# Sums and remainders at the entry of two feed-forward parts, moved from VectorE to GpSimd for three row pairs of four

## The reference

```python
# first block, after its mixer
x = x + jnp.einsum("bsc,cd->bsd", mix, w_out[l])
h = rms_norm(x, norm_ffn[l])
ff = jnp.square(jax.nn.relu(jnp.einsum("bsd,df->bsf", h, w_ff1[l])))
x = x + jnp.einsum("bsf,fd->bsd", ff, w_ff2[l])

# second block, after its mixer
mix = jnp.einsum('bsd,de->bse', merged, w_o)
x = layer_norm(ALPHA * x + mix, ln1_g, ln1_b)
hid = jax.nn.silu(jnp.einsum('bsd,df->bsf', x, w_gate)) * jnp.einsum('bsd,df->bsf', x, w_up)
ffn = jnp.einsum('bsf,fd->bsd', hid, w_down)
```

## Time and profile before

| | us |
|---|---|
| median of 3 runs | 2751.3 (2751.22 to 2753.59) |
| span of the profiled execution | 2749.3 |
| PE busy | 2639.2 (96%) |
| DVE busy | 1640.7 (60%) |
| ACT busy | 860.2 (31%) |
| POOL busy | 362.3 (13%) |

### The profile page before, as it was taken

One profiled execution on the slowest core, in us unless ns is written; L12 is line 12 of the kernel. 1 busy time (PEld: TensorE's weight loads), 2 busy tenths in 40 slices (PEclk: granted clock), 3 DMA queues, 4 the chain that ended last, 5 costly groups with the idle time before them and its releaser, 6 DMA issues. The chain is left out here.

```text
span 2749.3 us, 35644 instructions
## 1 busy us (share of the span) xinstructions
PE 2639.2 (96%) x14290; PEld 2108.7 (77%) x14290; DVE 1640.7 (60%) x2537; ACT 860.2 (31%) x1522; POOL 362.3 (13%) x191
## 2 busy tenths in 40 slices
PE   7999999999899999999999999999969999998998
PEld 5875558874488888888888888868967888887887
DVE  5894997771765655444783355323276666666446
ACT  4344444320444443111131222232143232323121
POOL 1212634420000000000011121144200000000000
PEclk9999999999899999999999999999989999999999
DMA  4011032230133337232121222262322222226131
GB/s 158 31 63 69 27 123 94 94 135 27 69 115 119 104 107 285 79 120 77 50 89 51 73 81 71 69 211 69 123 77 66 89 77 85 89 80 222 68 117 62
DMA packets 192627, 262.22 MB, mean 95 GB/s; under 512 B 15824, under 2 KB 121680, under 8 KB 192080
## 3 DMA queue, kind: packets, MB, share of 16 engines
q1 hardware_dynamic: 192464, 259.95, 28.0%
HBM read 196.80 MB, written 61.93 MB: 94 GB/s over the span
## 5 line engine op out<-in xcount | busy, mean ns | idle before, releaser
L1251 PE MATMUL ps<-gl_t,gl_slot 128*128 128x512 f32 x1056 | 243.0, 389 | 0.0
L1251 PEld LDWEIGHTS ps<-gl_t,gl_slot 128*128 128x128 f32 x1056 | 198.2, 188 | 41.2
L1251 PE MATMUL ps<-gl_b,gl_slot 128*128 128x512 f32 x768 | 182.7, 396 | 18.4 <-DVE gl_slot L3576 18.4
L1251 PE MATMUL ps<-w_hi,ff_hi 128*128 128x512 f32 x480 | 187.2, 390 | 0.0
L1251 PE MATMUL ps<-w_hi,ff_lo 128*128 128x512 f32 x480 | 186.8, 389 | 0.0
L1251 PE MATMUL ps<-w_lo,ff_hi 128*128 128x512 f32 x480 | 186.7, 389 | 0.0
L1251 PEld LDWEIGHTS ps<-gl_b,gl_slot 128*128 128x128 f32 x768 | 147.0, 192 | 50.1 <-issue 14.4
L1251 PE MATMUL ps<-ff_t,slot 128*128 128x512 f32 x768 | 179.3, 393 | 4.4 <-DVE ff_t L3017 4.4
L1251 PE MATMUL ps<-H_hi,tw_hi 128*128 128x512 f32 x448 | 175.6, 392 | 0.0
L1251 PE MATMUL ps<-H_rest,tw_hi 128*128 128x512 f32 x448 | 174.4, 389 | 0.0
L1251 PE MATMUL ps<-H_hi,tw_lo 128*128 128x512 f32 x448 | 174.3, 389 | 0.0
(11 more groups left out here) (420 smaller groups left out, 5678.2 us busy)
## 6 DMA issues: line engine op xcount, KB each, us to landing
wraw<-in_w_ff SPq DMA_DIRECT2D x32, 1024.0 KB, 5.9
ff_rows<-quad SPq DMA_DIRECT2D x64, 256.0 KB, 2.0
ff_raw<-ff_rows SPq DMA_DIRECT2D x7, 2048.0 KB, 7.9
traw<-in_w_in SPq DMA_DIRECT2D x28, 512.0 KB, 4.2
wq_raw<-in_w_in SPq DMA_DIRECT2D x6, 2048.0 KB, 8.6
wraw<-in_w_gate SPq DMA_DIRECT2D x22, 512.0 KB, 4.0
wraw<-in_w_up SPq DMA_DIRECT2D x22, 512.0 KB, 5.3
hid_rows<-gl_up SPq DMA_DIRECT2D x44, 256.0 KB, 2.0
```

The costliest lines, as they stand in the source:

```text
L1251: mm = nc.tensor.matmul(out_ap, stationary(a, k), moving(c, k), start=(k == 0 and n == 0), stop=(k == kts - 1 and n == 2))
```

## The change

For the row pairs 0, 1 and 2 of both entries, the two differences (t4 and t3 plain) and the four remainders leave DVE's queue and stand in POOL's, in the functions `pair_terms` and `gl_pair_terms`, with the same waits. For the last pair they stay on DVE (`last_terms`, `gl_last_terms`), right behind the lo of b22, as they stood. ACT's and PE's queues are as before, and so are the semaphores' counts.

```diff
+            def pair_terms(j):
+                hi_at = FEAT[0] + 7 * j + 2
+                cols, upper_cols = slice(P * j, P * j + P), slice(512 + P * j, 512 + P * j + P)
+                pool.wait_ge(sums_made, 3 * j + 1)
+                for h in (1, 0):
+                    G.tensor_tensor(half_plain[j][h], t2_plain, half_plain[j][h], ALU.subtract).then_inc(sums_made, 1)
+                pool.wait_ge(feat_hi, hi_at + 2)
+                G.tensor_tensor(ff_t1[:, 1, :, cols], t1_plain, ff_t1[:, 0, :, cols].bitcast(F32), ALU.subtract
+                                ).then_inc(terms_lo, 1)
+                pool.wait_ge(feat_hi, hi_at + 3)
+                pool.wait_ge(sums_made, 3 * j + 3)
+                G.tensor_tensor(ff_t4[:, 1, :, cols], half_plain[j][1], ff_t4[:, 0, :, cols].bitcast(F32), ALU.subtract
+                                ).then_inc(terms_lo, 1)
+                pool.wait_ge(feat_hi, hi_at + 4)
+                G.tensor_tensor(ff_t3[:, :, upper_cols], half_plain[j][0], ff_t3[:, :, cols].bitcast(F32), ALU.subtract
+                                ).then_inc(terms_lo, 1)
+                pool.wait_ge(feat_hi, hi_at + 5)
+                pool.wait_ge(terms_lo, 4 * j + 3)
+                G.tensor_tensor(ff_t2[:, j, 1], t2_plain, ff_t2[:, j, 0].bitcast(F32), ALU.subtract).then_inc(terms_lo, 1)
+            for j in range(3):
+                pair_terms(j)
...
                 elif q > 0:
                     term_sums(q // 2 - 1)
                     scale_row(q)
-                    rest_terms(q // 2 - 1)
...
             term_sums(3)
-            rest_terms(3)
+            last_terms(3)
...
                     gl_term_sums(t - 4)
-                    gl_rest_terms(t - 4)
+                    if t == NT - 1:
+                        gl_last_terms(t - 4)
```

More of the change, by code:

```diff
@@ L2558, in _, with gl_pair_terms @@
                 rest_wo(c)
+            def gl_pair_terms(j):
+                hi_at = FEAT[2] + 7 * j + 2
+                cols, upper_cols = slice(P * j, P * j + P), slice(512 + P * j, 512 + P * j + P)
+                pool.wait_ge(sums_made, GL_T_SUMS + 3 * j + 1)
+                for h in (1, 0):
+                    G.tensor_tensor(gl_half[j][h], gl_t2_plain, gl_half[j][h], ALU.subtract).then_inc(sums_made, 1)
+                pool.wait_ge(feat_hi, hi_at + 2)
+                G.tensor_tensor(gl_t1[:, 1, :, cols], gl_t1_plain, gl_t1[:, 0, :, cols].bitcast(F32), ALU.subtract
+                                ).then_inc(terms_lo, 1)
+                pool.wait_ge(feat_hi, hi_at + 3)
+                pool.wait_ge(sums_made, GL_T_SUMS + 3 * j + 3)
+                G.tensor_tensor(gl_t4[:, 1, :, cols], gl_half[j][1], gl_t4[:, 0, :, cols].bitcast(F32), ALU.subtract
+                                ).then_inc(terms_lo, 1)
+                pool.wait_ge(feat_hi, hi_at + 4)
+                G.tensor_tensor(gl_t3[:, :, upper_cols], gl_half[j][0], gl_t3[:, :, cols].bitcast(F32), ALU.subtract
+                                ).then_inc(terms_lo, 1)
+                pool.wait_ge(feat_hi, hi_at + 5)
+                pool.wait_ge(terms_lo, GL_TERMS + 4 * j + 3)
+                G.tensor_tensor(gl_t2[:, j, 1], gl_t2_plain, gl_t2[:, j, 0].bitcast(F32), ALU.subtract).then_inc(terms_lo, 1)
+            for j in range(3):
+                gl_pair_terms(j)
         @block.vector
@@ L2996, in term_sums, with last_terms @@
                                 ff_b22[:, :, P * j:P * j + P].bitcast(F32), ALU.subtract).then_inc(drained[b], 1)
+            def last_terms(j):
+                hi_at = FEAT[0] + 7 * j + 2
+                cols, upper_cols = slice(P * j, P * j + P), slice(512 + P * j, 512 + P * j + P)
                 dve.wait_ge(sums_made, 3 * j + 1)
@@ L2999, in term_sums @@
                 V.tensor_tensor(half_plain[j][0], t2_plain, half_plain[j][0], ALU.subtract).then_inc(sums_made, 1)
-            def rest_terms(j):
-                hi_at = FEAT[0] + 7 * j + 2
-                cols, upper_cols = slice(P * j, P * j + P), slice(512 + P * j, 512 + P * j + P)
                 dve.wait_ge(feat_hi, hi_at + 2)
@@ L3526, in gl_term_sums, with gl_last_terms @@
                                 gl_b22[:, :, P * j:P * j + P].bitcast(F32), sub).then_inc(drained[b], 1)
+            def gl_last_terms(j):
+                hi_at = FEAT[2] + 7 * j + 2
+                cols, upper_cols = slice(P * j, P * j + P), slice(512 + P * j, 512 + P * j + P)
                 dve.wait_ge(sums_made, GL_T_SUMS + 3 * j + 1)
@@ L3529, in gl_term_sums @@
                 V.tensor_tensor(gl_half[j][0], gl_t2_plain, gl_half[j][0], sub).then_inc(sums_made, 1)
-            def gl_rest_terms(j):
-                hi_at = FEAT[2] + 7 * j + 2
-                cols, upper_cols = slice(P * j, P * j + P), slice(512 + P * j, 512 + P * j + P)
                 dve.wait_ge(feat_hi, hi_at + 2)
```

## The result

The changed kernel takes 2756.75 us (median of 19 runs, 2754.32 to 2764.22) against 2751.55 us of the kernel before on the same chips (19 runs, 18 of them from 2749.05 to 2755.3, and one of 3008.72 that the median doesn't feel): ratio 1.002 with a 95% interval of 1.0014 to 1.0026. It is 5.2 us slower, just under the 0.2% that was set as the line, and so on the side that the prediction calls "same". The forecast was 2758.7, with 2752 to 2762 around it: the sign and the range held, the size was 7.4 instead of 5.2 us.

What follows compares the result with a forecast made beforehand. The loop over VectorE and ACT, not VectorE's busy time, was taken to bound the entries. First entry 2.8 plus second 4.6 gave 7.4 us: 2749.3 becomes 2756.7, the median 2.0 above it, 2758.7; range 2752 to 2762.

Steps and rivals of the forecast that it cites:

- What bounds: Both entries: PE waits for the loop over VectorE and ACT, 17.8 us per two tiles in the first, not VectorE's busy time.
- GpSimd's pace, 6.3 us from t2_plain to the cast: Each moved pair: five GpSimd instructions, 4 x 1.23 + 1.29 = 6.2 us, plus 0.1 hand-over, before ACT's cast of t2.
- Second entry, 1.9 + 2.7 = 4.6: Lo of the first weights 4.6 us later: 1.9 from late squares in pairs 0 and 1, 2.7 from pair 2's late cast.
- First entry, 2.8: First entry 2.8 us slower: 3 x 0.45 from late squares, plus one fall of the granted clock at 1.4.
- 0.45 late per pair: First entry: squares at 697.2 instead of 696.76, behind ACT's cast that waits for GpSimd, in each of three pairs.
- The price of the fall of the granted clock, 1.4: First entry: low clock after PE's new stall adds 1.4 us to the loop; possible in pairs 0 and 1, taken once.
- The collision itself: First entry: root and scaling instructions with two SBUF inputs wait for GpSimd's current instruction; small ones up to 1.2 us, scaling 2 or more.
- PE's new stall: First entry: PE waits some 2.5 us for the scaling before its turn, covered by losing the later 2.30 us stall.
- the first `ff_b` product 1.4 to 4.2 us later than 736.56: Sign for the changed profile: the first entry's first product comes 1.4 to 4.2 us later than 736.56.
- rival 1: VectorE and GpSimd don't meet in small instructions: first entry -3.0, second +4.6, together +1.6 us, 2752.9; chance 0.16.
- Rival 2: ACT isn't held, VectorE's freed time counts: 5.7 and 12.9 us gained, 2732.7, chance 0.05; in-between case 2747.1, chance 0.09.
- The chances: Whole kernel: slower by over about 0.2% (5.5 us) 0.55, same 0.40, faster 0.05.

Runs made afterwards that it cites:

- the kernel with pair 2 on VectorE: The move in the second entry only, pair 2 back on VectorE, GpSimd making pairs 0 and 1: 2753.5 us against 2750.7 of the kernel before.
- the kernel with t1 last: Both entries: differences on VectorE, GpSimd's t1 remainder after t4's and t3's; second entry: squares before t2's cast, pair 2 on VectorE. 2750.8 us against 2751.1 before.
- the kernel with t1 last in the second entry alone: Second entry only: differences on VectorE, t1's remainder after t4's and t3's, squares before t2's cast, pair 2 on VectorE. 2748.9 us against 2751.1 before.

## Why the prediction held, and where not

- **What bounds:** held. The loop over VectorE and ACT sets the entries, and of the 26 us of VectorE's time that was to be freed none came off.
- **GpSimd's pace, 6.3 us from t2_plain to the cast:** held, 2015.97 to 2022.38 is 6.4. The spacing of 1.23 in it was read from a multiplication (the eight rows of L2515), not, as the text says, from the same kind of subtraction; the subtractions then followed each other at 1.22 to 1.26.
- **Second entry, 1.9 + 2.7 = 4.6:** held. The length says 4.47, the kernel with pair 2 on VectorE 1.83 and so 0.92 for each of the others and 2.62 for pair 2.
- **First entry, 2.8:** this is the term that was mis-sized; it measured 0. Two steps of it failed. The squares "0.45 late per pair" were on time: I had let each small VectorE instruction hold GpSimd for 0.1, and the record shows GpSimd's first four instructions at 1.25 to 1.26, so the cast came at 696.2 in the time of before and not at 696.7. The price of the fall of the granted clock, 1.4, did not come: the stalls of 2.10 and 1.77 us left the turn at 1.09 and the next product at 7.03. The fall came behind the third stall, where it cost nothing. Both are seen in one execution of the changed kernel and in one of that with the first entry alone; that such a fall can cost the loop 1.7 us is shown by the kernel with t1 last.
- **The collision itself:** held, with its mechanism. Three small instructions at 0.66, 1.20 and 1.00 and the scaling at 2.25 were foretold ("up to 1.2", "2 us or more"), and they went when GpSimd was held back. What the scaling takes from GpSimd's remainder of t3, 1.0 us, reaches the cast and the squares. It eats what the earlier drain would have given, to within 0.03 us, and that the two are equal is luck: no row said so. The Trainium skill's page "SBUF — State Buffer", section "Who interferes with whom", which the prediction cites, also names VectorE's 2-port modes as meeting GpSimd, so the "only" in that sentence is too narrow; no run here shows such an instruction.
- **PE's new stall:** held, 2.10 against 2.5, and so did what was said of its cover: the later one is gone. But the sign "the first `ff_b` product 1.4 to 4.2 us later than 736.56" looks fulfilled by 738.48 only because the entry started 1.98 us later.
- **Rivals:** rival 1 (no meeting in the small instructions) is out. Rival 2 needs GpSimd's results in about 2 us; out. The sum for "ACT isn't held" in it was too hopeful as well: with the squares freed, the kernel gained 1.3 per pair and not 4.3, because VectorE then meets GpSimd.
- **The chances:** 0.55 stood on slower by over 0.2%, 0.40 on the same. At 5.2 us, or 0.19%, the result lies on the line between them, just on the side of the smaller chance.

In sum: forecast 2.8 + 4.6 = 7.4, by the lengths -0.1 + 4.5 = 4.4, by the medians 5.2. The 4.4 lies inside the interval of the ratio (3.9 to 7.2 us); the other 0.8 is not explained by any row. The second entry carries the result by the mechanism that was foretold, and the range was wide enough to hold the miss in the first.

## What to carry to other kernels

Moving work off a busy engine gains only if what waits for that work doesn't get it later: count the instructions that stand between the input and the first one who waits, at the price of the new engine, and look at what stands behind the waiter in its queue. Here VectorE got 4.3 us back per pair and spent 6.7 waiting for ACT. When the move is made all the same, give the slow engine only what nobody waits for soon, put the waiter's other work ahead of its wait (worth 4.4 us here), and leave the last item, which has nothing behind which to hide, on the fast engine (2.6 us here).

## What the runs showed of the hardware

- A VectorE instruction with two SBUF inputs that finds GpSimd at work waits for the end of GpSimd's current instruction, at each size seen: 128x1 took 0.66 to 1.22 us instead of 0.16, in nine kernels, 128x512 up to 1.28 instead of 0.68 (and 4.69 beside a GpSimd instruction of 4.61), and 128x1024 up to 2.25 instead of 1.28. The instructions between them with one SBUF input (L2628 and L2631 in the changed kernel) stayed at 0.15, and those with one input in PSUM and one in SBUF (L3043) at 0.68. The other way, GpSimd's instruction is not measurably longer for a small one of VectorE (1.26) and 1.0 longer for one of 128x1024 (2.26).
- Collisions are moved rather than removed by reordering: in the second entry the remainder of t1 first stretched a difference by 0.6 and one instruction of the root by 0.9, t1 last stretched two of the root by 0.9 each; in the first entry t1 last stretched the scaling by 1.0.
- The granted clock doesn't follow from a stall's length alone. Six kernels have the first entry as it was, with a first stall of 2.30 to 2.31 us. In three the clock fell right behind it, and the turn took 1.43, 1.45 and 1.64 us. In the other three that turn took 1.09 and the product behind it 7.03; the clock fell behind the next stall instead. One of these is the kernel with t1 last in the second entry alone:

```profile
704.06 1.09 PE L1245 MATMUL ps<-sb 128*128 128x128 f32 x8 [2.30 <-DVE sb L3196]
...
721.85 1.09 PE L1245 MATMUL ps<-sb 128*128 128x128 f32 x8 [2.09 <-DVE sb L3196]
722.78 8.73 PE L1556 MATMUL ps<-sb 128*128 128x512 f32 x16
```

  From 724 to 726 us its granted clock was 0.50. Its entry was 737.57 - 686.13 = 51.44 us, that of before 51.28: wherever in this loop the fall came, it had nearly the same length, as VectorE and ACT set it. Behind which of the two stalls a run gets it stays open.
